# Gathering expert results at the end of a layer: two early lower rows instead of three, own semaphores for the lower rows, row numbers sorted later

## What is computed

```python
g_w, g_idx = lax.top_k(softmax(xt @ w_group + b_group), 1)
e_in = the four logits of that group
e_val, e_idx = lax.top_k(e_in, 2)
e_w = softmax(e_val) * g_w
hid = silu(xt @ w_gate[e]) * (xt @ w_up[e])      # for the two experts e of the token
out = sum over the two experts of e_w * (hid @ w_down[e])
x = x + gt_m * out                               # the residual
y = rms_norm(x, final_norm)                      # after the second layer
```

## Time and profile before

| | us |
|---|---|
| median of 3 runs (lowest, highest) | 1293.39 (1291.4, 1294.76) |
| the profiled execution, in all | 1292.7 |
| its span, first to last instruction | 1290.9 |
| TensorE busy in it | 1231.8 (95%) |
| VectorE busy | 589.3 (46%) |
| ScalarE busy | 409.8 (32%) |
| GpSimd busy | 58.2 (5%) |

### The profile page before, as it was taken

One profiled execution on the slowest core, in us unless ns is written; L12 is line 12 of the kernel. 1 busy time (PEld: TensorE's weight loads), 2 busy tenths in 40 slices (PEclk: granted clock), 3 DMA queues, 4 the chain that ended last, 5 costly groups with the idle time before them and its releaser, 6 DMA issues.

```text
span 1290.9 us, 17251 instructions
## 1 busy us (share of the span) xinstructions
PE 1231.8 (95%) x5561; PEld 681.9 (53%) x5562; DVE 589.3 (46%) x1338; ACT 409.8 (32%) x855; POOL 58.2 (5%) x63
## 2 busy tenths in 40 slices
PE   7999999999999999998978999799999999999997
PEld 4554566666664475443434444466654574444443
DVE  1322455555552574322228544888735663322216
ACT  2332344444451121111022325677732111111122
POOL 0103000000000020000002000000000110000002
PEclk9999999999999999999998999899999999999999
DMA  9979999622244057999987000600020279999947
GB/s 373 414 312 407 414 413 410 259 100 100 100 186 165 33 202 244 355 355 356 364 313 267 9 1 9 256 1 1 2 99 0 102 274 317 355 293 334 352 183 265
DMA packets 88357, 290.18 MB, mean 225 GB/s; under 512 B 9209, under 2 KB 27580, under 8 KB 86876
## 3 DMA queue, kind: packets, MB, share of 16 engines
q1 hardware_dynamic: 46032, 185.68, 39.4%
q0 software_dynamic: 16640, 64.59, 12.7%
q10 hardware_dynamic: 25612, 38.96, 8.9%
HBM read 214.48 MB, written 74.73 MB: 224 GB/s over the span
## 4 chain that ended last, share of the span: by engine, by line
PE 80%; DMA 6%; DVE 5%; ACT 3%; SPq 3%; issue 2%; ACTq 1%; DVEq 1%; POOL 0%; POOLq 0%
PE ps L2114 16%; PE ps L1724 11%; PE ps L1741 10%; PE ps L2143 7%; PE ps L1666 7%; PE ps L1994 6%; PE ps L1957 4%; PE ps L1769 3%; PE ps L2193 3%; PE ps L1818 3%; PE ps L1686 2%; DMA arena<-in_moe_gu 2%; PE ps L2056 2%; PE ps L1950 2%; PE ps L1967 2%
## 5 line engine op out<-in xcount | busy, mean ns | idle before, releaser
L2114 PE MATMUL ps<-arena 128*128 (+1 forms) x560 | 247.7, 595 | 0.0
L2114 PEld LDWEIGHTS ps<-arena 128*128 128x128 f32 x560 | 104.5, 191 | 118.1 <-issue 118.0
L1666 PE MATMUL ps<-const,arena 128*128 128x128 f32 (+2 forms) x1000 | 145.4, 279 | 18.0 <-DMA const<-in_const 8.2
L1724 PE MATMUL ps<-arena 128*128 128x512 f32 (+2 forms) x400 | 152.1, 535 | 4.6 <-DVE arena L1246 1.2
L1666 PEld LDWEIGHTS ps<-const,arena 128*128 128x128 f32 (+2 forms) x1000 | 115.8, 142 | 76.6 <-issue 39.8
L1139 DVE TENSOR_REDUCE hst<-ps 128x1 f32<-128x640 f32 (+1 forms) x160 | 110.9, 714 | 94.0 <-PE ps L1994 80.1
L1741 PE MATMUL ps<-arena 128*128 128x512 f32 x320 | 142.0, 597 | 1.4 <-issue 1.4
L2143 PE MATMUL ps<-arena 128*128 (+1 forms) x280 | 126.1, 593 | 2.2 <-ACT arena L844 2.2
L721 ACT ACTIVATE arena<-ps,hst 128x640 f32<-128x640 f32 (+1 forms) x160 | 112.4, 706 | 42.0 <-DVE hst L1139 42.0
L1724 PEld LDWEIGHTS ps<-arena 128*128 128x128 f32 x400 | 74.4, 190 | 74.1 <-issue 58.1
L1741 PEld LDWEIGHTS ps<-arena 128*128 128x128 f32 x320 | 59.1, 190 | 69.8 <-issue 69.7
(11 more groups left out here) (218 smaller groups left out, 1173.9 us busy)
## 6 DMA issues: line engine op xcount, KB each, us to landing
arena<-in_moe_gu SPq DMA_DIRECT2D x128, 512.0 KB, 13.1
arena<-in_ada_w SPq DMA_DIRECT2D x62, 768.0 KB, 11.9
slot_rows<-arena POOLq DMA_DIRECT2D x10, 4096.0 KB, 67.7
arena<-in_moe_w_down SPq DMA_DIRECT2D x64, 512.0 KB, 16.1
slot_rows<-arena ACTq DMA_DIRECT2D x33, 512.0 KB, 8.5
arena<-slot_rows ACTq DMA_DIRECT2D x124, 128.0 KB, 13.4
arena<-mod_rows SPq DMA_DIRECT2D x12, 512.0 KB, 12.3
arena<-in_gqa_w_qkv SPq DMA_DIRECT2D x12, 512.0 KB, 13.7
```

The source lines that it names most:

```text
L1666: return nc.tensor.transpose(out, in_, ident[0:rows, 0:rows])
L1724: last = mm(bank(2 + b, cols), hT[l](t)[:, k * P:(k + 1) * P], w[:, k], start=k == 0, stop=k == KD - 1)
L2114: last = mm(bank(gu_bank(u)), e_xsT[:, nth(u, D)][:, k * P:(k + 1) * P], w(k * BANK, BANK), start=k == 0, stop=k == KD - 1)
```

## The change

Four things are changed together.

- `GATHERS` has a new order: (0,1) moves from fourth to third place, (1,1) from sixth to fifth, and (2,0) and (3,0) go behind them. Two gathers are issued before `last_stored`, not three.
- The low rows get three semaphores of their own (`low_gathered0` to `2`, tile t uses t mod 3), the high rows keep `gathered{t}`. A high gather no longer waits for its tile's low one; low gathers 3 and 4 wait for low 0 and 1.
- `place_rows` converts the two row numbers unsorted, in one instruction. `order_weights` sorts those of all five tiles into a new tensor `slot_s`, which the gathers use, behind a new semaphore `ordered`.
- In `last_sums` tile 3's residual, with its wait for `last_stored`, moves behind (1,1), and VectorE waits for `norm_row` one step earlier.

```diff
-GATHERS = ((0, 0), (1, 0), (2, 0), (0, 1), (3, 0), (1, 1), (2, 1), (4, 0), (3, 1), (4, 1))
-GATHERS_EARLY = 3
+GATHERS = ((0, 0), (1, 0), (0, 1), (2, 0), (1, 1), (3, 0), (2, 1), (4, 0), (3, 1), (4, 1))
+GATHERS_EARLY = 2
+LOW_SEMS = 3
...
     def gathered(l, t, high):
-        return S(f"gathered{t}"), 32 * l + 16 * high + 16
+        if high:
+            return S(f"gathered{t}"), 16 * (l + 1)
+        early = t % LOW_SEMS
+        n = (NTILE - 1 - early) // LOW_SEMS + 1
+        return S(f"low_gathered{early}"), 16 * (n * l + t // LOW_SEMS + 1)
...
+            pool.wait_ge(S("ordered"), l + 1)
             pool.wait_ge(S("fourth_stored"), 16 * (l + 1))
             pool.wait_ge(S("early_stored"), 32 * (l + 1))
             for n, (t, high) in enumerate(GATHERS):
                 if n == GATHERS_EARLY:
                     pool.wait_ge(S("last_stored"), 32 * (l + 1))
-                if high:
-                    pool.wait_ge(*gathered(l, t, 0))
-                rows, at = (e_low[t], e_high[t])[high], 2 * t + high
+                if not high and t >= LOW_SEMS:
+                    pool.wait_ge(*gathered(l, t - LOW_SEMS, 0))
+                rows, at = (e_low[t], e_high[t])[high], high * NTILE + t
...
             op(nc.vector.tensor_reduce(pl, split(t2, 2), AX.X, ALU.add))
-            settle()
-            nc.vector.tensor_tensor(slot_i[:, 2 * t:2 * t + 1], pl[:, 0:1], pl[:, 1:2], ALU.min)
-            nc.vector.tensor_tensor(slot_i[:, 2 * t + 1:2 * t + 2], pl[:, 0:1], pl[:, 1:2], ALU.max).then_inc(S("slotted"), 1)
+            op(nc.vector.tensor_copy(slot_i[:, 2 * t:2 * t + 2], pl)).then_inc(S("slotted"), 1)
...
         def order_weights():
...
+            nc.vector.tensor_tensor(slot_s[:, 0:NTILE], rows[:, :, 0], rows[:, :, 1], ALU.min)
+            nc.vector.tensor_tensor(slot_s[:, NTILE:], rows[:, :, 0], rows[:, :, 1], ALU.max).then_inc(S("ordered"), 1)
...
         experts(1)
-        for n in range(6):
+        for n in range(5):
             gate_next(n)
         dve.wait_ge(S("final_landed"), 16)
+        gate_next(5)
         final(0)
...
-            for t in range(LAT):
-                if t == LAT - 1:
-                    pe.wait_ge(S("last_stored"), 32 * 2)
+            for t in range(LAT - 1):
                 part(t, xt(t), True)
             for n, (t, high) in enumerate(GATHERS):
+                if (t, high) == (LAT - 1, 0):
+                    pe.wait_ge(S("last_stored"), 32 * 2)
                 if (t, high) == (LAT, 0):
                     pe.wait_ge(S("y_ready"), 1)
-                    part(LAT, xt(LAT), True)
+                if t >= LAT - 1 and not high:
+                    part(t, xt(t), True)
```

More of the change, by code:

```diff
@@ L211, in program @@
     arena = sb("arena", ARENA)
-    slot_i = sb("slot_i", 2 * NTILE, I32)
+    slot_i, slot_s = sb("slot_i", 2 * NTILE, I32), sb("slot_s", 2 * NTILE, I32)
     plan = sb("plan", 4 * SLOT_TILES + NE + 1, I32)
@@ L656, in _ @@
                     pool.wait_ge(S("last_stored"), 32 * (l + 1))
-                if high:
-                    pool.wait_ge(*gathered(l, t, 0))
-                rows, at = (e_low[t], e_high[t])[high], 2 * t + high
-                pool.indirect_dma_start(rows, None, slots, bass.IndirectOffsetOnAxis(ap=slot_i[:, at:at + 1], axis=0))\
-                    .then_inc(S(f"gathered{t}"), 16)
+                if not high and t >= LOW_SEMS:
+                    pool.wait_ge(*gathered(l, t - LOW_SEMS, 0))
+                rows, at = (e_low[t], e_high[t])[high], high * NTILE + t
+                pool.indirect_dma_start(rows, None, slots, bass.IndirectOffsetOnAxis(ap=slot_s[:, at:at + 1], axis=0))\
+                    .then_inc(gathered(l, t, high)[0], 16)
     @block.scalar
```

## The result

| | before | after |
|---|---|---|
| median of 15 runs each (lowest, highest), us | 1291.4 (1290.42, 1294.76) | 1294.09 (1291.99, 1297.04) |
| span of the profiled execution, us | 1290.9 | 1292.9 |
| mean granted clock of TensorE in it | 0.989 | 0.992 |

The ratio is 1.0016, with an interval from 1.0009 to 1.0024: the change costs 2.1 us (1.2 to 3.1; the two medians are 2.7 us apart). The time of 1293.8 that was predicted lies 0.3 from the measured median. That is luck: the three runs shown of before had a median of 1293.39, all 15 have 1291.4, and the step predicted was +0.45 us where it is +2.1. The two errors nearly cancel.

What follows compares the result with a forecast made beforehand. TensorE, busy for 95% of the span, was taken as the bound, so only its waits count. End +0.35, seam 0 and routing +0.1 made +0.45 us, giving 1293.8 us as the median, range 1291.4 to 1296.3.

Steps and rivals of the forecast that it cites:

- The issue of (0,1) stays: End of layer 1: the gather of tile 0's higher expert row is still issued at 1261.84, if the last store lands unchanged.
- (1,0) lands earlier, since (2,0) no longer shares with it: End of layer 1: tile 1's lower-row gather lands near 1263.4 instead of 1264.3; TensorE waits 1.04 us for it.
- (0,1) takes 4.4 us: End of layer 1: tile 0's higher-row gather lands 4.4 us after issue instead of 6.29; TensorE waits 1.13 us.
- The rival of a slow landing: Tile 0's higher-row gather keeps 5 to 6.29 us because of norm row and last store; about +1.7 us, 1295.1; chance 0.18.
- The fast landing: Tile 0's higher-row gather lands within 3.3 to 4.0 us in both layers; about -0.9 us, 1292.5; chance 0.24.
- No wait from (0,1) on: End of layer 1: behind tile 0's higher row TensorE always has work, ten parts or 17.16 us without waiting.
- The wait for the final scaling goes: End of layer 1: TensorE's 1.23 us wait before tile 2's higher row, behind VectorE's final scaling of tile 0, disappears.
- The seam, 0: Between the layers: the new gather order changes nothing, 0 us, bounds 0.33 won and 1.9 lost.
- The routing, +0.1: Ahead of each layer's experts: row-number conversion takes 0.51 us instead of 0.46, +0.05 in each layer, +0.1 us in all.
- The clock: Rival, end of layer 1: TensorE's waits drop its clock, 4 us at half speed cost 2 us more; 1295.8; chance 0.05.

Runs made afterwards that it cites:

- e12: The kernel after, with the final norm's row loaded early by SP instead of behind the last store; ratio 1.0024.
- e7: The kernel before, with SP loading the final norm's row ahead of layer 1's experts instead of ScalarE behind the last store; ratio 0.9998.
- e8: The kernel before, with the final norm's row loaded early by SP and the seventh scaling of gathered rows ahead of tile 0's final scaling; ratio 0.9991.
- e9: The kernel before, with e8's early norm row and scaling order, layer 0's last three gathers held until the next projection's second weight block landed; ratio 0.9980.
- e10: The kernel after, with the old order of gathers, VectorE's scalings and TensorE's parts in layer 1 alone; ratio 1.0011.
- e11: The kernel after, with the old order of gathers, three of them early, in layer 0 alone; ratio 1.0021.
- e6_hold: The kernel after, with GpSimd holding layer 0's last three gathers until the next projection's second weight block has landed; ratio 1.0014.
- e2_free: The kernel before in its old order, with separate semaphores for low rows, so no high gather waits for its tile's low one; ratio 1.0008.

## Why the prediction was right and wrong

The forecast was a change within 0.3%, and it is one, and the time lies in the range. The sum behind it was too small: +0.45 us against +2.1, below the interval's 1.2, and outside the -0.1 to +0.9 that had half of the chances. By its steps:

- **The issue of (0,1) stays.** Right. It was issued 5.86 us after the first gather, 6.02 before.
- **(1,0) lands earlier, since (2,0) no longer shares with it.** Wrong in size. On the scale of before the estimate was 1263.4 (bounds 1263.1 and 1264.3). (1,0) took 6.9 us instead of 7.2, which is 1264.0 on that scale (0.99 earlier than its own). In the five more kernels with two early gathers and the late row it took 6.6 to 7.2, in the four with three 7.1 to 7.8: the gain is some 0.5 us, not 0.9. Its company was the last store and the norm's row on q10 (58% and 35% of the engines in the rows above). Without that row and with two early gathers it took 5.8 (e12); with three, 5.6 to 6.6 (e7, e8, e9). The step divided the bytes of GpSimd's queue by that queue's rate as if (1,0) had the engines for itself, and left the other queue out. TensorE waits 1.43 us there and not 1.04. In the sum this costs nothing, since (0,1) lands later still.
- **(0,1) takes 4.4 us.** Near: 4.8, and 4.8 to 5.0 in five more kernels. The wait was 0.75 and not 1.13, since TensorE came later by the steps ahead. Up to here it is 3.27 us against the 3.05 predicted, and (0,1) alone sets it: 0.4 us more latency, 0.16 less by the earlier issue. The rival of a slow landing, 5 to 6.29 us because of the norm's row, falls by its own condition (the 5.0 of three kernels is its lowest value), although its price of +1.7 is closer to the result. The fast landing falls as well.
- **No wait from (0,1) on.** Wrong by 0.47 us, and one of the prediction's own signs of being wrong. (2,0) and (1,1) follow at GpSimd's pace, but (0,1)'s issue took 1.29 us and not 0.97, (2,0) landed 5.2 us and (1,1) 5.9 us after its issue, and VectorE has 1.28 us to do between landing and TensorE. With the old order (2,0) had long landed by then, and TensorE had 1.72 us of work in it.
- **The wait for the final scaling goes.** Right, 36 instructions without a break. The sum at the end is 3.74 against 2.70: **+1.04** instead of +0.35, and 1.05 over the groups of kernels.
- **The seam, 0.** The part on VectorE was small, as said: 0.2 us. But the projection's weights, which the prediction left to "wait for this landing too, as before", have less margin than it assumed: TensorE needs the second block at some 25.3 us, and it lands at 24.8 to 27.7 where nothing is held. The prediction looked at what starts that load and not at what shares the engines with it.
- **The routing, +0.1.** The place itself was right (0.06 against 0.05). Up to the last feeding matmuls it costs 0.08 and 0.17 us in the two layers, so +0.25.
- **The clock.** The rival falls. TensorE's windows in the kernel after (length, busy, granted clock, DMA share, GB/s):

```profile
1262.00:1264.00 2.00, 1.07 (x3) 1.00 1.01 410
1264.00:1266.00 2.00, 1.18 (x3) 1.00 0.68 170
1266.00:1268.00 2.00, 1.65 (x4) 1.00 0.95 336
```

The clock stayed at 1.00, 2.4 GHz, with TensorE at work for little over half of the first 4 us.

So 1.05 + 0.25 = 1.3 us of the 2.1 have a place that several kernels show. The 0.8 left are of the size of the seam's mean difference in the profiles (1.26 - 0.34 = 0.92, or 0.8 with the start of the first matmul), and the times of e10 and e11 don't confirm it. **Open** is what the change costs at the seam on average. The steps that failed are thus the waits behind (0,1) and its landing at the end (0.7 us together), the routing's size (0.15), and, not shown, the seam that was put at nothing.

## What to carry to other kernels

Before a transfer is moved ahead of another to make it land sooner, count what its successor did as cover: here (0,1) won 1.5 us of latency and lost 3.43 us of ready work ahead of it. Look for what shares the DMA engines on every queue, not only on the one that is reordered; moving one 512 KB load off the critical moment gave about the same and kept the cover. Where two queues are loaded and one of them carries what is needed first, holding the other one's issue can take the wait away, as e6_hold and e9_both show at the seam. That the whole kernel gains by it is likely and not shown.

## What the runs showed of the hardware

- The time from issue to landing of a 512 KB gather depends on both neighbours at once. (0,1) in layer 1 took 5.9 to 6.3 us with three gathers ahead and the norm's row behind the last store, 4.8 to 5.0 with two ahead, 4.4 to 5.0 with three ahead and no norm's row, and 4.7 with two ahead and no row (one run). Taking away either gives all of the gain, the second gives nothing more. In that last run no DMA engine moved anything from 0.8 to 1.9 us after the start of the issue, which took 1.27 us (the window above): that part of the latency is there with empty queues too.
- None of the gathers looked at landed in under 4.3 us (layer 0's (0,1) in e2_free). The Trainium skill, DMA: Bandwidth & Descriptors, Anatomy of one DMA, gives 2.0 us plus the bytes at 436 GB/s, by which I estimate 3.2 us for these; the runs disagree, in the kernel after too, where the 20 gathers are, from least to most:

```profile
DMA to landing us min/median/max: 4.8/5.9/15.1
```

- An indirect DMA's issue on GpSimd takes 0.93 to 1.06 us mostly, but 1.29 to 1.66 in five of layer 1's ten in the kernel after, where the one behind it starts that much later; before, two of ten took 1.86.
